# Band attention: masked scores in three buffers in turn instead of two

## The reference

```
def gqa_attend(q, k, v, sink=None):            # the context tokens
    s = einsum('bqhgd,bkhd->bhgqk', q, k) * d ** -0.5
    p = softmax(concatenate([s, s_sink], -1))[..., :-1]
    o = einsum('bhgqk,bkhd->bqhgd', p, v)

def banded_window_attention(q, k, v, k_ctx, v_ctx, sink):   # the 512 tokens
    valid = (abs(kpos - qpos) <= WINDOW) & (kpos >= 0) & (kpos < t)
    s_win = where(valid, einsum(qn, kn) * scale, -inf)      # 3 blocks of 128 keys
    s_ctx = einsum(qn, k_ctx) * scale                       # all 256 context keys
    p = softmax(concatenate([s_win, s_ctx, s_sink], -1))
    o = p[..., :nw] @ vn + p[..., nw:nw + n_ctx] @ v_ctx
```

## Time and profile before

| | us |
|---|---|
| median of 3 runs | 2608.44 |
| lowest and highest | 2606.38, 2612.1 |
| the profiled execution | 2603.68 |
| its span, first to last instruction | 2601.9 |
| mean granted TensorE clock of the span | 0.955 of full |
| band attention in it, 1152.89 to 1273.60 | 120.7 |

### The profile page before, as it was taken

The page is one execution under the profiler, slowest core; times in us unless marked ns, Lnnn a source line. Parts: engine busy times, 40 slices in busy tenths (PEclk is TensorE's granted clock), DMA queues, the critical chain, the costliest instruction groups (busy, mean ns, idle before and its releaser), DMA issues. The chain is left out here.

```text
span 2601.9 us, 35012 instructions
## 1 busy us (share of the span) xinstructions
PE 2377.1 (91%) x14323; PEld 1927.4 (74%) x14323; DVE 1222.1 (47%) x1930; ACT 794.8 (31%) x1301; POOL 1065.0 (41%) x728
## 2 busy tenths in 40 slices
PE   6987688999997989967889999999989999899998
PEld 5866466777775779855678888888877688688887
DVE  4517627856564670467426242332427752423422
ACT  4232424433335422334332121111124363322221
POOL 2325224655553322324235343343425124555553
PEclk8998897999998999979999999999989999899999
DMA  8470122544442112100113224333311101223231
GB/s 267 154 234 1 59 65 95 177 134 154 151 148 75 33 49 65 33 1 1 33 49 98 79 89 141 104 124 114 97 57 49 49 1 53 69 90 97 97 97 49
DMA packets 224701, 229.95 MB, mean 88 GB/s; under 512 B 7375, under 2 KB 221219, under 8 KB 224547
## 3 DMA queue, kind: packets, MB, share of 16 engines
q1 hardware_dynamic: 224211, 227.66, 27.2%
q10 hardware_dynamic: 336, 0.11, 0.0%
HBM read 225.65 MB, written 2.10 MB: 88 GB/s over the span
## 5 line engine op out<-in xcount | busy, mean ns | idle before, releaser
L1266 POOL TENSOR_TENSOR w_lo<-ring,w_hi 128x1024 fp32r<-128x1024 f32 x128 | 311.8, 2436 | 430.6 <-ACT w_hi L1261 430.6
L2073 DVE SCALAR_TENSOR_TENSOR xT<-ps,mods,xT 128x512 f32<-128x512 f32 (+1 forms) x160 | 108.5, 683 | 541.0 <-PE ps L1327 500.6
L1261 ACT ACTIVATE w_hi<-ring 128x1024 fp32r<-128x1024 f32 x128 | 135.7, 1060 | 737.9 <-PE ps L1327 701.8
L1325 PE MATMUL ps<-hidden_hi,w_hi 128*128 128x512 f32 (+1 forms) x768 | 273.9, 357 | 5.5 <-POOL hidden_lo L2436 5.5
L1326 PE MATMUL ps<-hidden_lo,w_hi 128*128 128x512 f32 (+1 forms) x768 | 272.1, 354 | 0.0
L1327 PE MATMUL ps<-hidden_hi,w_lo 128*128 128x512 f32 (+1 forms) x768 | 271.6, 354 | 0.0
L2359 DVE SCALAR_TENSOR_TENSOR ffn_sums<-ps,cols,ffn_sums 128x441 f32<-128x441 f32 (+2 forms) x352 | 215.0, 686 | 105.5 <-ACT ffn_sums L2280 105.5
L1325 PE MATMUL ps<-h_hi,w_hi 128*128 128x512 f32 (+1 forms) x720 | 256.3, 356 | 6.7 <-POOL w_lo L1266 3.0
L1326 PE MATMUL ps<-h_lo,w_hi 128*128 128x512 f32 (+1 forms) x720 | 255.0, 354 | 0.0
L1327 PE MATMUL ps<-h_hi,w_lo 128*128 128x512 f32 (+1 forms) x720 | 254.6, 354 | 0.0
L2426 DVE TENSOR_TENSOR squares<-squares 128x512 f32<-128x512 f32 (+1 forms) x72 | 145.1, 2015 | 217.1 <-ACT squares L2412 217.1
(11 more groups left out here) (438 smaller groups left out, 5257.3 us busy)
## 6 DMA issues: line engine op xcount, KB each, us to landing
ring<-in_mlp_w SPq DMA_DIRECT2D x64, 1024.0 KB, 5.3
ring<-in_ada_w SPq DMA_DIRECT2D x48, 1024.0 KB, 5.3
ring<-in_w_ada SPq DMA_DIRECT2D x24, 1024.0 KB, 9.6
ring<-in_ffn_w_up SPq DMA_DIRECT2D x22, 1024.0 KB, 7.1
ring<-in_ab_w_in SPq DMA_DIRECT2D x11, 1024.0 KB, 5.2
ring<-in_ffn_w_down SPq DMA_DIRECT2D x12, 768.0 KB, 5.9
ring<-in_w_in SPq DMA_DIRECT2D x8, 1024.0 KB, 7.7
ring<-in_c_w_in SPq DMA_DIRECT2D x6, 1024.0 KB, 5.0
```

What stands on the lines that cost most here:

```text
L1261: act.activation(w_hi[m][:, 0:x["kt"], :], ring[:, x["n"] % NS, 0:x["kt"], m * P:(m + 1) * P], ACT.Copy).then_inc(SW["w_hi"].sem, 1)
L1266: pool.tensor_tensor(w_lo[m][:, 0:x["kt"], :], ring[:, x["n"] % NS, 0:x["kt"], m * P:(m + 1) * P], w_hi[m][:, 0:x["kt"], :].bitcast(F32), ...
L1325: pe.matmul(o, w_hi[m][:, k, :], h, start=(k == 0), stop=False)
L2073: return nc.vector.scalar_tensor_tensor(x, bank, column_of(gates, t * 2 + 2 * gate + r), x, ALU.mult, ALU.add)
```

## The change

The masked scores get a third buffer. All indices of `sc`, of the maxima and of the denominators go from `p % 2` to `p % 3`, and `top(p)` waits for the transposes of pair p-3 instead of p-2. The sink's column is written for n < 3 instead of n < 2, since there are three buffers to write: eight small copies more in all. For room, `sc` (now 6 x 641 columns) runs past the end of the recurrence's key tile, whose place it had; of the four weight tiles of the projection behind, the two high ones move to where the two low ones were, and the two low ones go to `oa`, the output gate.

```diff
@@ turn, TensorE
-                                                   sc[:, p % 2, e, 1 + c * P:1 + (c + 1) * P], ident)
+                                                   sc[:, p % 3, e, 1 + c * P:1 + (c + 1) * P], ident)
@@ top, VectorE
                         wait(dve, "qk", p + 1)
-                        if p >= 2:
-                            wait(dve, "turned", 2 * (p - 1))
+                        if p >= 3:
+                            wait(dve, "turned", 2 * (p - 2))
                         for e in range(2):
                             h = 2 * hp + e
-                            if n < 2:
-                                dve.tensor_copy(sc[:, p % 2, e, 0:1], nsink[:, h:h + 1])
+                            if n < 3:
+                                dve.tensor_copy(sc[:, p % 3, e, 0:1], nsink[:, h:h + 1])
                             sig(dve.tensor_tensor_reduce(
-                                sc[:, p % 2, e, 1:1 + width], flat[:, at_of(n, e):at_of(n, e) + width],
+                                sc[:, p % 3, e, 1:1 + width], flat[:, at_of(n, e):at_of(n, e) + width],
                                 bands[:, m0 * CH:m0 * CH + width], -scale, nsink[:, h:h + 1], ALU.add, ALU.min,
-                                tops[:, 2 * (p % 2) + e:2 * (p % 2) + e + 1]), "top")
+                                tops[:, 2 * (p % 3) + e:2 * (p % 3) + e + 1]), "top")
@@ norm, VectorE
-                            b = 2 * (p % 2) + e
+                            b = 2 * (p % 3) + e
...
-                            sig(dve.tensor_scalar(sc[:, p % 2, e, 1:1 + width], sc[:, p % 2, e, 1:1 + width],
+                            sig(dve.tensor_scalar(sc[:, p % 3, e, 1:1 + width], sc[:, p % 3, e, 1:1 + width],
@@ expo, ScalarE
-                            b = 2 * (p % 2) + e
+                            b = 2 * (p % 3) + e
...
-                            sig(act.activation(sc[:, p % 2, e, 0:1 + width], sc[:, p % 2, e, 0:1 + width], ACT.Exp,
+                            sig(act.activation(sc[:, p % 3, e, 0:1 + width], sc[:, p % 3, e, 0:1 + width], ACT.Exp,
@@ where the tiles lie
+        at_oa = used[0]
         oa = part(4 * TOK, "p (t n) -> p t n", t=4)
...
-        free_k = k_tok.rearrange("p c n -> p (c n)")
+        scores_at = big[:, free0 - NCH * 512:free0 - NCH * 512 + 6 * (5 * CH + 1)]
         ab_made = Made("ab_out", rounded("ab_out_hi", big_at, [P, KT, TOK]), h_hi,
-                       BOTH, [big_at + 4 * (24576 - (4 - i) * KT * P) for i in range(4)])
+                       BOTH, [big_at + 4 * at for at in (24576 - 2 * KT * P, 24576 - KT * P, at_oa, at_oa + KT * P)])
...
-                       free_k[:, 0:4 * (5 * CH + 1)].rearrange("p (b e n) -> p b e n", b=2, e=2),
+                       scores_at.rearrange("p (b e n) -> p b e n", b=3, e=2),
...
-                       squares.rearrange("p a n -> p (a n)")[:, 0:7 * CH], small[:, 0:4], small[:, 4:12], small[:, 12:16],
+                       squares.rearrange("p a n -> p (a n)")[:, 0:7 * CH], small[:, 0:6], small[:, 6:14], small[:, 14:20],
```

More of the change, by code:

```diff
@@ L3357, in program @@
             R[n].close(v)
-        free_k = k_tok.rearrange("p c n -> p (c n)")
+        scores_at = big[:, free0 - NCH * 512:free0 - NCH * 512 + 6 * (5 * CH + 1)]
         ab_made = Made("ab_out", rounded("ab_out_hi", big_at, [P, KT, TOK]), h_hi,
-                       BOTH, [big_at + 4 * (24576 - (4 - i) * KT * P) for i in range(4)])
-        assert free0 - NCH * 512 + 4 * (5 * CH + 1) <= 24576 - 4 * KT * P
+                       BOTH, [big_at + 4 * at for at in (24576 - 2 * KT * P, 24576 - KT * P, at_oa, at_oa + KT * P)])
+        assert free0 - NCH * 512 + 6 * (5 * CH + 1) <= 24576 - 2 * KT * P
         band_attention(qb, kb, vb, hT,
-                       free_k[:, 0:4 * (5 * CH + 1)].rearrange("p (b e n) -> p b e n", b=2, e=2),
+                       scores_at.rearrange("p (b e n) -> p b e n", b=3, e=2),
                        ka.rearrange("p t n -> p (t n)")[:, 0:4 * 5 * CH].rearrange("p (b e n) -> p b e n", b=2, e=2),
-                       squares.rearrange("p a n -> p (a n)")[:, 0:7 * CH], small[:, 0:4], small[:, 4:12], small[:, 12:16],
+                       squares.rearrange("p a n -> p (a n)")[:, 0:7 * CH], small[:, 0:6], small[:, 6:14], small[:, 14:20],
                        [(hT[:, t, :], oa[:, t, :]) for t in range(4)], ab_made)
```

## The result

The changed kernel takes 2587.76 us in the median (4 runs, 2585.66 to 2589.33), beside 2610.27 us for the kernel before on the same chip (2606.38 to 2614.14). The ratio is 0.992, with a 95% interval from 0.9901 to 0.9939: 22.5 us less, between the medians, by the interval 16 to 26 us (the ratio itself stands for 21 us). The profiled execution took 2588.51 us (span 2586.7) against 2603.68: 15.2 us less. Forecast were 2593.3 us and a gain of 15.1, with a range of 2585.5 to 2601.

A forecast was written before the change was run, and what follows sets the result against it. TensorE was taken to bound the kernel, and engines waiting for each other the band attention. Saving 0.69 us a pair over 22 waits gave 15.1 us: 2608.44 less 15.1 is 2593.3 us, range 2585.5 to 2601.

The forecast's parts named there:

- Which wait: Band attention: the maximum's 22 waits for the transposes, 30.6 us, would go; the wait left is always met.
- The six steps: Band attention, maximum to maximum into blocks 0 to 5: 3.42, 3.46, 4.37, 3.72, 3.46, 2.94 us; round 21.37 against 25.49.
- The steps into 1 and 2: Maximum, then next scores, then their maximum, sharing one PSUM place: 3.46 us into block 1, 4.37 into block 2.
- the step into 3: Into block 3, VectorE's own work sets the pace: maximum, two sink copies, normalisation and copy, 3.72 us.
- 15.1 us for the stage: Band attention stage: 22 waits taken away, 0.69 us a pair, 15.1 us saved; stage 105.6 us long.
- first pairs at the lower clock: Start of the band attention: all paths stretch at the lower clock; the clocks differ by less than one step's saving.
- my mean of 0.69 a pair: Band attention: 4.12 us saved a round of six pairs, taken as 0.69 us for each pair.
- what lies behind the stage: Projection after the band attention: starts from the same signals, counted at nothing.
- my main case: Whole kernel: gain of 11 to 21 us, chance 0.62.
- a chance of 0.06: Whole kernel: gain of more than 21 us, as held normalisations and cold stretches vanish, 2587; chance 0.06.
- a danger for the new rhythm only: TensorE at the lower clock all through the stage: about 155 us, some 35 us slower, 2643; slower by over 5.2: 0.04.
- GpSimd's hold: GpSimd holds VectorE's normalisations: 6.0 us paid already, up to 13.7 more lost, gain 1.4; within 5.2 us: 0.10.

The follow-up runs named there:

- e2: Changed kernel, but the maximum again waits for the transposes two pairs back: 2609.20 us, ratio 1.0001 to the kernel before.
- e3: Changed kernel without any wait of the maximum for the transposes: 2584.67 us, ratio 0.9907 to the kernel before.
- e5 to e8: Four more matmuls a pair, then a VectorE reduction a pair, each in the changed kernel and the kernel before: 2589.64, 2610.48, 2592.51, 2617.13 us.
- e5: Changed kernel with four more matmuls (0.5 us) ahead of the values of each pair: 2589.64 us, ratio 0.9935 to the kernel before.
- e7: Changed kernel with a VectorE reduction over 512 columns behind each normalisation: 2592.51 us, ratio 0.9940 to the kernel before.

## Why the prediction was right, point by point

**Which wait, and that it goes.** Right: 22 waits gone (rows above), e2 brings them and the time back, e3 shows that the one left costs nothing.

**The six steps.** Right: 21.37 us walked, 20.97 measured, no step more than 0.14 us off. The steps into 1 and 2 are 0.12 and 0.14 us too long in the walk because of the hop of 0.14 us that I put behind the scores: in the changed kernel the scores of block 1 run from 1206.08 for 1.69 us, to 1207.77, and VectorE goes on at 1207.80. I had taken that hop without a row that shows it. e5 to e8 confirm which engine stands in which step, with two near misses: the step into 3 has more room on TensorE than I thought, and the step into 1 less.

**15.1 us for the stage.** Mis-sized by 4 us. The largest part is the first pairs at the lower clock, of which I said that the two clocks differ by less than one step's saving. The maxima of pairs 1, 2 and 3 in the kernel before,

```profile
1160.73 0.15 DVE L2835 COPY big<-small 128x1 f32<-128x1 f32 x1 [3.04 <-PE ps L2777]
...
1168.89 0.89 DVE L2836 CUSTOM_DVE_ANT_0 big<-ps,squares,small 128x640 f32<-128x640 f32 x1 [5.14 <-PE ps L2789]
...
1175.05 0.75 DVE L2836 CUSTOM_DVE_ANT_0 big<-ps,squares,small 128x512 f32<-128x512 f32 x1 [2.54 <-PE ps L2789]
```

and in the changed one,

```profile
1160.42 0.15 DVE L2835 COPY big<-small 128x1 f32<-128x1 f32 x1 [3.04 <-PE ps L2777]
...
1166.56 0.15 DVE L2835 COPY big<-small 128x1 f32<-128x1 f32 x1 [3.12 <-PE ps L2777]
...
1170.46 0.75 DVE L2836 CUSTOM_DVE_ANT_0 big<-ps,squares,small 128x512 f32<-128x512 f32 x1 [0.16 <-PE ps L2777]
```

are 14.32 and 10.04 us apart. Two steps saved 4.3 us where the walk has 1.9 and my mean of 0.69 a pair 1.4. Two things speak for the reason. At the lower clock TensorE's work is longer, the scores of block 2 for one 4.23 us against 2.33, so taking the transposes out of the circle should be worth more there. And the changed kernel left the lower clock sooner: from 1168 to 1174 us the kernel before still had 0.50 and the changed one a mean of 0.82. These two rows, before and after:

```profile
1168.00:1174.00 6.00, 4.09 (x19) 2.87 (x18) 3.55 (x9) 2.25 (x5) 0.00 (x0) 0.50 0.00 0
1168.00:1174.00 6.00, 5.99 (x45) 3.95 (x44) 5.70 (x17) 3.79 (x10) 0.85 (x3) 0.82 0.00 0
```

The sum over all 22 steps, by the starts of the maxima, is 19.3 us. The saving of each step at full clock, as measured, gives 17.6 of it: the round saves 0.4 us more than walked, and the 22 steps hold only three into 0, which saves nothing, so the mean of 0.69 was 1 us too low by itself. The steps of pairs 2 to 9, at the lower clock or beside GpSimd's wide instructions, saved 4.0 us more than that. Against it stands the interference around L661, where two steps took 10.46 us against 8.60 before, 2.6 us worse than at full clock without a hold. The last 0.3 us is one step into block 1 that was slower before than the others.

**The profiled time.** 2588.5 against a forecast of 2588.6 is agreement by luck: the stage saved 19 us and the stages behind it, the projection at first, gave 4 back, some of it through a lower clock. I had counted what lies behind the stage at nothing.

**The median.** The gain, 22.5 and 21.5 us between the medians, 21 and 23 by the ratios, lies at the upper end of my main case, which reached to 21 us, or beyond it, where I had put a chance of 0.06. The forecast of 2593.3 us was 5.5 us too high. What the sum has no term for is that the old rhythm may be the more exposed to the lower clock. I had this the wrong way round as a rival, as a danger for the new rhythm only, and took the profile of before, with 27 us at the lower clock, as the usual case; e2 shows the same rhythm at 48. How often it falls there is not known.

**GpSimd's hold.** The rival was real but no loss: L2848 went from 29.5 to 30.5 us. What was paid already was a little more than the 6.0 us of the sum: free of a hold the three widths take 0.35, 0.49 and 0.55 us, 22.2 us for all 48 and not 23.5. I had priced the hold for what it could take back, and not as a gain of its own. It was worth half as much as the change.

By the Trainium skill ("SBUF — State Buffer", "Who interferes with whom") a `tensor_scalar` between SBUF tiles can need the ports that VectorE shares with GpSimd and is then blocked until the instruction that came first ends, and an operation with at most one SBUF input, outside the two-port modes, is not. This trace agrees on both: the normalisations ended 0.2 to 0.3 us behind the two L661, and the maximum, with one of its two inputs in PSUM, took 0.47 us beside them.

## What to carry to other kernels

Where three engines hand a tile round in a circle, walk one round, step by step, with each engine's own work and each resource that exists once (here one place for scores in PSUM) as a path, and take the last; at full clock a buffer more is worth what the longest path falls by, and no more. An engine that waits much may still stand in every step, so test it by adding work to it. Look beside the chain for long instructions that hold a short one, and for matmuls in pairs of unequal width: cutting the first took 10.9 us off and the second 6.9, beside 21.5 for the buffer.

## What the runs showed of the hardware

- The same kind of idle stretch on TensorE is followed by the lower clock in one execution and not in another. With it busy 2.52 of 4 us the next 4 us had a granted clock of 0.54 (e2); with it busy 2.17 of 4 at the same place they had 1.00 (kernel before). With 0.5 us of matmuls more in every pair (e5) the stage's mean clock was 0.92, not 0.87, and the stage 1.5 us longer; with VectorE's load instead (e7) it was 0.90.
- Two GpSimd `tensor_tensor` of 2.4 us each held two VectorE `tensor_scalar` of 0.49 us to 1.64 and 2.39 us; with GpSimd's instructions in pieces of 256 columns the 48 normalisations took 4.9 us less in all.
- Two matmuls side by side on different rows of the array took about the time of the wider: 512 beside 128 and 128 beside 512 columns 2.33 us, the same work cut alike 1.36, of which some 0.3 us may be a wait between them.
- Code that no edit touched moves by several us between executions: the stage begins at 1145.6 us in e3 and at 1152.9 in the kernel before. A gain smaller than that in one profiled execution has to be read in its own stage.
